# Inverse of the RWKV-7 chunk matrices: four block levels computed on the columns of the odd blocks only

## The chip, the cores and the metric

The kernel runs on one core of one Trainium2 chip. The metric is the device time of one execution in microseconds, as a median of several runs. The engines are called TensorE (PE), VectorE (DVE), ScalarE (ACT), GpSimd (POOL) and SyncE (SP, which only issues loads here).

## What is computed

The reference is a two-layer decoder trunk on 256 tokens of width 2048. Each layer has three head groups side by side (a gated linear recurrence, latent attention, RWKV-7 time mixing), an output projection and a SwiGLU feed-forward part. The part that matters here is the RWKV-7 state update, 8 heads of 64:

```python
def step(state, inp):
    r_t, w_t, k_t, v_t, kk_t, a_t = inp
    sa = jnp.einsum('bhvk,bhk->bhv', state, -kk_t)
    state = (state * w_t[:, :, None, :]
             + sa[..., :, None] * (kk_t * a_t)[..., None, :]
             + v_t[..., :, None] * k_t[..., None, :])
    return state, jnp.einsum('bhvk,bhk->bhv', state, r_t)
```

The kernel does it in 4 chunks of 64 tokens. Within a chunk the dependence of sa on earlier sa of the chunk is a unit lower triangular 64x64 matrix for each head, and it needs that matrix's inverse: 8 heads by 4 chunks, 32 inverses a layer.

## The kernel before

Two heads share the 128 partitions (rows 0 to 63 and 64 to 127), so a tile of 128 x 16 x 64 holds all 32 matrices; h8 is a half of it, 8 matrices wide. The inverse is built by doubling blocks. `inv` holds the inverse of the diagonal blocks of size m, `inv_t` its transpose. For m = 2, 4, 8, 16, 32 (RW_LEVELS, levels 0 to 4) and for each half:

1. GpSimd (L435) masks `mab` to the blocks below the diagonal that join two neighbouring blocks of size m (odd block of rows, even block of columns) into `rw_level`. It begins when TensorE has finished level_g of the level before (rw_gt_mm).
2. TensorE, level_g(k), multiplies `rw_level` (stationary) with `inv_t` (moving) into bank 0 or 1. L1715 is the line of the helper `both_heads`, two products for each of 8 matrices. An f32 product is two instructions, so a level_g or level_x with both halves is 64 instructions. L1724 is the helper for the last level.
3. ScalarE, gt_out(k) at L680, copies the bank into `g_t`.
4. TensorE, level_x(k), multiplies `inv` (stationary) with `g_t` (moving) into bank 2 or 3.
5. VectorE, level(k), subtracts the bank from `inv_t` (L1280) and transposes the result in 64x64 blocks into `inv` (L1272).

The last level (m = 32) already works on its quarters only. Every operation is released by semaphores, and the order on each engine is written out by hand. All engines have attention work between the levels. On TensorE the order is level_g(0), k_turn(1) (L1640), level_x(0), attend(1), attend(2) (L1670 and L1676), level_g(1), attend(3), level_x(1), p_turn(0), p_turn(1) (L1688), level_g(2), level_x(2), p_turn(2), p_turn(3), mix(0) (L1696 and L1697), level_g(3), mix(1), product, level_x(3), product, level_g(4), and so on. On VectorE it is k_norm(1) (L1171 and L1173), a small product at L1301, score_max(0) (addition L1183 of PSUM scores and mask, maxima L1186, small products L1190), level(0), score_max(1), probs(0) (reciprocal L1198, products L1202), score_max(2), probs(1), score_max(3), level(1), probs(2), probs(3), level(2), and so on. A score addition L1183 needs the attend of its pair of heads; p_turn needs probs of its pair.

Of the kernel before, what the change touches and what calls it, by code (L numbers as in the profile page):

```python
# [32 lines left out]
ACT = mybir.ActivationFunctionType  # L33
# [8 lines left out]
CH = 512  # L42
# [11 lines left out]
RC = 64  # L54
# [31 lines left out]
RW_LEVELS = [2, 4, 8, 16, 32]  # L86
# [26 lines left out]
def build(nc, stream, x_in, positions, params, consts, lora, gains, rows, out):  # L113
    with ExitStack() as ctx:
# [3 lines left out]
        def sem(name):  # L118
            return ctx.enter_context(nc.semaphore(name))
# [30 lines left out]
        def at(off, *shape):  # L150
            n = int(np.prod(shape))
            assert off + n <= ARENA
            v = arena[:, off:off + n]
            if len(shape) == 2:
                return v.rearrange("p (a b) -> p a b", b=shape[1])
            if len(shape) == 3:
                return v.rearrange("p (a b c) -> p a b c", b=shape[1], c=shape[2])
            return v
# [65 lines left out]
        rw_level = gain[:, 1024:2048].rearrange("p (n i) -> p n i", i=RC)  # L224
# [3 lines left out]
        g_t = at(RING_END + 9856, JC, RC)  # L228
        inv = at(RING_END + 10880, JC, RC)
        inv_t = at(RING_END + 11904, JC, RC)  # L230
# [10 lines left out]
        y_out = at(RING_END + 10880, 4, SEQ)  # L241
        UP_BANK = [4, 6, 4, 4, 6, 6, 4, 6]
        EVEN, ODD = slice(0, 64), slice(64, 128)

        UPPER = [slice(0, 32), slice(64, 96)]
        LOWER = [slice(32, 64), slice(96, 128)]

        psum = ctx.enter_context(nc.psum_tensor("psum", [P, 8, CH], F32))

        def bank(b, n=1):  # L250
            return psum[:, b:b + n, :].rearrange("p a b -> p (a b)")
# [36 lines left out]
        def S(name):  # L288
            if name not in names:
                names[name] = sem(name)  # L290
            return names[name]
# [151 lines left out]
        def _(act):  # L443
# [60 lines left out]
            for l in range(DEPTH):  # L504
# [164 lines left out]
                def gt_out(k):  # L669
                    last = k == len(RW_LEVELS) - 1  # L670
                    for hf in range(2):
                        h8 = slice(8 * hf, 8 * hf + 8)
                        act.wait_ge(S("rw_gt_mm"), 10 * l + 2 * k + hf + 1)
                        if last:
                            g3 = bank(hf).rearrange("p (n t) -> p n t", n=8)
                            nc.scalar.activation(g_t[UPPER[0], h8, 32:64], g3[UPPER[0], :, 32:64], ACT.Copy)
                            nc.scalar.activation(g_t[UPPER[1], h8, 32:64], g3[UPPER[1], :, 32:64], ACT.Copy).then_inc(
                                S("rw_gt_ready"), 1)
                        else:
                            nc.scalar.activation(g_t[:, h8, :].rearrange("p a b -> p (a b)"), bank(hf),  # L680
                                                 ACT.Copy).then_inc(S("rw_gt_ready"), 1)

                up_out(0)
                scaled(4, 12, 2, 0)
# [57 lines left out]
                nc.scalar.activation(rkT, bank(4)[:, 0:SEQ], ACT.Copy).then_inc(S("mla_rT_ready"), 1)  # L742
                stacked(1, b_st, 0)
                gt_out(0)
                k_out(1)
                softmax(0)
                softmax(1)
                gt_out(1)
                softmax(2)
                softmax(3)  # L750
                probs_out(0)
                probs_out(1)
                gt_out(2)
                probs_out(2)
                probs_out(3)
# [83 lines left out]
        def _(dve):  # L839
# [9 lines left out]
            def u(ins):  # L849

                steps[0] += 1
                ins.then_inc(chain, 1)

            def settle():

                dve.wait_ge(chain, steps[0])

            def vs(ins, name, value):

                ins.then_inc(S(name), 1)  # L860
                dve.wait_ge(S(name), value)

            tt, ts, stt = nc.vector.tensor_tensor, nc.vector.tensor_scalar, nc.vector.scalar_tensor_tensor
            red, rec, cp = nc.vector.tensor_reduce, nc.vector.reciprocal, nc.vector.tensor_copy
            ADD, SUB, MUL, MAX = ALU.add, ALU.subtract, ALU.mult, ALU.max
# [93 lines left out]
            for l in range(DEPTH):  # L959
# [73 lines left out]
                flat = "p h t -> p (h t)"  # L1033
# [236 lines left out]
                def turn_blocks(dst, src):  # L1270

                    return nc.vector.transpose(dst.rearrange("p n t -> p (n t)"), src.rearrange("p n t -> p (n t)"))  # L1272

                def level(k):
                    last = k == len(RW_LEVELS) - 1
                    for hf in range(2):
                        h8 = slice(8 * hf, 8 * hf + 8)
                        dve.wait_ge(S("rw_dinv_mm"), 10 * l + 2 * k + hf + 1)
                        if not last:
                            vs(tt(inv_t[:, h8, :], inv_t[:, h8, :], bank(2 + hf).rearrange("p (n t) -> p n t", n=8), SUB),  # L1280
                               "rw_xt", 12 * l + 2 * k + hf + 3)
                            vs(turn_blocks(inv[:, h8, :], inv_t[:, h8, :]), "rw_x", 10 * l + 2 * k + hf + 3)
                        else:
                            d3 = bank(2 + hf).rearrange("p (n t) -> p n t", n=8)
                            for up in UPPER:
                                z = inv_t[up, h8, 32:64]
                                u(tt(z, z, d3[up, :, 32:64], SUB))
                            settle()
                            dve.sem_inc(S("rw_xt"), 1)
# [11 lines left out]
                v(tt(md[:, :, 0:3], hd[:, :, 0:3], hd[:, :, 1:4], MUL))  # L1301
                score_max(0)
                level(0)
                score_max(1)
                probs(0)
                score_max(2)
                probs(1)
                score_max(3)
                level(1)
                probs(2)  # L1310
                probs(3)
                level(2)
                mix_lo(0)
                mix_lo(1)
# [125 lines left out]
        def _(pe):  # L1440
# [50 lines left out]
            for l in range(DEPTH):  # L1491
# [218 lines left out]
                def both_heads(b0, ns, left, right, w):  # L1710

                    last = None
                    for m, n in enumerate(ns):
                        for hp in (EVEN, ODD):
                            last = mm(bank(b0, 2)[hp, m * w:(m + 1) * w], left(hp, n), right(hp, n),  # L1715
                                      start=True, stop=True)
                    return last

                def quarters(b0, ns, left, right):

                    last = None
                    for m, n in enumerate(ns):
                        for h in range(2):
                            last = mm(bank(b0)[UPPER[h], m * RC + 32:(m + 1) * RC], left(h, n), right(h, n),  # L1724
                                      start=True, stop=True)
                    return last
# [5 lines left out]
                def tile_of(z):  # L1732
                    return lambda hp, n: z[hp, n, :]

                def unit_of(hp, n):
                    return idst[hp, :]

# [6 lines left out]
                def level_g(k):  # L1744
                    last = k == len(RW_LEVELS) - 1
                    pe.wait_ge(S("rw_level_ready"), 5 * l + k + 1)
                    for hf in range(2):
                        ns = range(8 * hf, 8 * hf + 8)
                        pe.wait_ge(S("rw_xt"), 12 * l + 2 * k + hf + 1)
                        if last:  # L1750
                            quarters(hf, ns, lambda h, n: rw_level[LOWER[h], n, 0:32],
                                     lambda h, n: inv_t[LOWER[h], n, 32:64]).then_inc(S("rw_gt_mm"), 1)
                        else:
                            both_heads(hf, ns, tile_of(rw_level), tile_of(inv_t), RC).then_inc(S("rw_gt_mm"), 1)

                def level_x(k):
                    last = k == len(RW_LEVELS) - 1
                    for hf in range(2):
                        ns = range(8 * hf, 8 * hf + 8)
                        pe.wait_ge(S("rw_gt_ready"), 10 * l + 2 * k + hf + 1)  # L1760
                        pe.wait_ge(S("rw_x"), 10 * l + 2 * k + hf + 1)
                        if not last:
                            both_heads(2 + hf, ns, tile_of(inv), tile_of(g_t), RC).then_inc(S("rw_dinv_mm"), 1)
                        else:
                            quarters(2 + hf, ns, lambda h, n: inv[UPPER[h], n, 0:32],
                                     lambda h, n: g_t[UPPER[h], n, 32:64]).then_inc(S("rw_dinv_mm"), 1)
# [12 lines left out]
                for t in range(TT):  # L1779
                    for j in range(4):  # L1780
                        n = 4 * t + j
# [135 lines left out]
                for n, (c, j) in enumerate(WO_ORDER):  # L1917
# [10 lines left out]
                    if n == 1:  # L1928
# [5 lines left out]
                        for m in range(JC):  # L1934
                            i, k = m % 4, m // 4
# [148 lines left out]
```

## Time and profile before

| | us |
|---|---|
| median of 3 runs | 2366.62 (2366.38 to 2368.61) |
| profiled execution | 2367.02 |
| its span | 2365.2 |
| TensorE busy | 2326.6 (98%) |
| VectorE busy | 1341.4 (57%) |
| ScalarE busy | 1082.8 (46%) |
| GpSimd busy | 64.3 (3%) |

The span is the time from the first to the last instruction. Busy is the time in which an engine has at least one instruction in work. The chain of waits goes back from the last instruction to whatever released it, so an operation on it is one whose length counts. TensorE holds 94% of that chain and VectorE 5%. The clock granted to TensorE is full in all 40 slices, and TensorE is busy for nine tenths or more in nearly all of them. The inverses lie between 299 and 347 us in layer 0 and between 1472 and 1521 us in layer 1.

### The profile page before, as it was taken

To read this page: it belongs to the slowest core of one execution; us is meant where nothing else is said; L and a number is where in the kernel's file an instruction comes from. 1 tells how busy PE (TensorE), PEld (TensorE's weight loads), DVE (VectorE), ACT (ScalarE), POOL (GpSimd) and SP (SyncE) were. 2 spreads that over 40 slices of the span, in tenths; PEclk is the share of its full clock that TensorE was granted. 3 is DMA by queue.
4 is the path that set the end of the run, shared out by engine and by line. 5 is a ranking of instruction groups with operands and counts; after the bars stand their busy time and mean duration, and the time that the engine had idled before them with its cause. 6 is when DMAs were issued, how large, how long until landed. Compare 5 with 4: busy or idle time off the path is not lost.

```text
span 2365.2 us, 34149 instructions
## 1 busy us (share of the span) xinstructions
PE 2326.6 (98%) x13908; PEld 1929.4 (82%) x13908; DVE 1341.4 (57%) x1369; ACT 1082.8 (46%) x1287; POOL 64.3 (3%) x67
## 2 busy tenths in 40 slices
PE   7999989999999999999999999999999999999999
PEld 6888678888888888888888886888888888888887
DVE  5696576644555444445556857675454554454454
ACT  5554654444443344444445546444444433444433
POOL 1000110000000000000000002100000000000000
PEclk9999999999999999999999999999999999999999
DMA  8453304655555555555454533055555555555553
GB/s 314 165 183 119 132 3 178 205 203 189 184 194 187 191 194 194 193 180 195 179 194 151 193 113 106 21 182 191 185 189 195 181 192 196 196 187 187 194 185 136
DMA packets 60179, 411.27 MB, mean 174 GB/s; under 512 B 6688, under 2 KB 6720, under 8 KB 13472
## 3 DMA queue, kind: packets, MB, share of 16 engines
q1 hardware_dynamic: 58624, 401.63, 47.2%
q0 software_dynamic: 1440, 7.97, 1.0%
q8 instruction: 88, 1.44, 0.2%
q14 instruction: 27, 0.22, 0.0%
HBM read 407.48 MB, written 2.10 MB: 173 GB/s over the span
## 4 chain that ended last, share of the span: by engine, by line
PE 94%; DVE 5%; issue 1%; ACT 0%; DMA 0%; DVEq 0%; POOL 0%; ACTq 0%; POOLq 0%
PE psum L1459 28%; PE psum L1461 28%; PE psum L1460 28%; PE psum L1620 2%; PE psum L1868 1%; PE psum L1715 1%; PE psum L1955 1%; PE psum L1470 1%; PE psum L1521 1%; DVE arena L1202 1%; DMA gain<-gains_dram 0%; DVE arena L1272 0%; DVE small L1186 0%; DVE arena L1183 0%; PE psum L1696 0%
## 5 line engine op out<-in xcount | busy, mean ns | idle before, releaser
L870 DVE TENSOR_TENSOR w_lo<-raw,w_hi 128x1024 fp32r<-128x1024 f32 (+2 forms) x752 | 901.6, 1205 | 841.6 <-ACT w_hi L453 834.7
L453 ACT ACTIVATE w_hi<-raw 128x1024 fp32r<-128x1024 f32 (+2 forms) x752 | 782.0, 1044 | 1099.2 <-PE psum L1461 1086.7
L1459 PE MATMUL psum<-w_hi,hT_hi 128*128 128x512 f32 (+2 forms) x2128 | 821.8, 386 | 3.8 <-DVE w_lo L870 2.5
L1461 PE MATMUL psum<-w_hi,hT_lo 128*128 128x512 f32 (+2 forms) x2128 | 816.6, 384 | 0.0
L1460 PE MATMUL psum<-w_lo,hT_hi 128*128 128x512 f32 (+2 forms) x2128 | 816.4, 384 | 0.0
L1459 PEld LDWEIGHTS psum<-w_hi,hT_hi 128*128 128x128 f32 x2128 | 399.8, 188 | 82.6 <-issue 2.5
L1461 PEld LDWEIGHTS psum<-w_hi,hT_lo 128*128 128x128 f32 x2128 | 399.8, 188 | 78.2
L1460 PEld LDWEIGHTS psum<-w_lo,hT_hi 128*128 128x128 f32 x2128 | 400.0, 188 | 76.5
L1459 PE MATMUL psum<-w_hi,act_hi 128*128 128x512 f32 x880 | 343.6, 390 | 0.0
L1461 PE MATMUL psum<-w_hi,act_lo 128*128 128x512 f32 x880 | 342.5, 389 | 0.0
L1460 PE MATMUL psum<-w_lo,act_hi 128*128 128x512 f32 x880 | 342.4, 389 | 0.0
L1461 PEld LDWEIGHTS psum<-w_hi,act_lo 128*128 128x128 f32 x880 | 165.2, 188 | 34.2
L1459 PEld LDWEIGHTS psum<-w_hi,act_hi 128*128 128x128 f32 x880 | 165.3, 188 | 34.0
L1460 PEld LDWEIGHTS psum<-w_lo,act_hi 128*128 128x128 f32 x880 | 165.3, 188 | 33.8
L1620 PE MATMUL psum<-raw,arena 128*128 128x384 f32 (+1 forms) x192 | 71.8, 525 | 2.0 <-ACT arena L634 1.3
L1620 PEld LDWEIGHTS psum<-raw,arena 128*128 128x128 f32 x192 | 35.4, 190 | 31.0 <-issue 13.7
L1393 DVE TENSOR_TENSOR act_lo<-psum,act_hi 128x1024 f32 (+1 forms) x22 | 26.9, 1225 | 37.8 <-ACT act_hi L820 37.8
L914 DVE TENSOR_TENSOR x<-x,psum 128x1024 f32<-128x1024 f32 x24 | 29.2, 1215 | 13.4 <-PE psum L1461 13.4
L1715 PE MATMUL psum<-arena 64*64 64x64 f32 x1024 | 32.4, 219 | 1.5 <-ACT arena L680 1.5
L1715 PEld LDWEIGHTS psum<-arena 64*64 64x64 f32 x1024 | 30.8, 135 | 3.4 <-ACT arena L680 1.8
L820 ACT ACTIVATE act_hi<-psum 128x1024 f32 (+1 forms) x22 | 22.6, 1028 | 20.8 <-PE psum L1955 20.8
L401 POOL TENSOR_TENSOR gain<-arena,row 128x128 f32<-128x128 f32 x2 | 0.9, 461 | 1034.2 <-PE psum L1604 1034.2
(312 smaller groups left out, 1213.0 us busy)
## 6 DMA issues: line engine op xcount, KB each, us to landing
raw<-stream_dram SPq DMA_DIRECT2D x360, 1024.0 KB, 4.8
raw<-stream_dram SPq DMA_DIRECT2D x16, 512.0 KB, 3.5
raw<-stream_dram SPq DMA_DIRECT2D x8, 768.0 KB, 4.5
raw<-stream_dram SPq DMA_DIRECT2D x8, 640.0 KB, 3.8
gain<-gains_dram POOLq DMA_DIRECT2D x3, 1024.0 KB, 6.9
x<-x_in_dram SPq DMA_DIRECT2D x4, 512.0 KB, 8.8
out_dram<-x SPq DMA_DIRECT2D x4, 512.0 KB, 5.5
lor<-lora_dram POOLq DMA_DIRECT2D x2, 832.0 KB, 12.0
```

The source lines that it names most:

```text
L453: nc.scalar.activation(w_hi[:, q % HALF_RING, 0:2 * w], raw[:, j % 4, hf * 2 * w:(hf + 1) * 2 * w], ACT.Copy).then_inc(hi_done, 1)
L870: tt(w_lo[:, q % HALF_RING, 0:2 * w], raw[:, j % 4, hf * 2 * w:(hf + 1) * 2 * w], w_hi[:, q % HALF_RING, 0:2 * w].bitcast(F32), SUB).then_ ...
L914: vs(tt(xs, xs, psum[:, b0:b0 + 2, :], ADD), "x_added", n_added)
L1202: u(tt(z, z, along(small[:, 64 + off + 2 * p:66 + off + 2 * p], n), MUL))
L1393: tt(act_lo[:, k, :], bank(4, 2).rearrange("p (k t) -> p k t", k=4), act_hi[:, k, :].bitcast(F32), SUB).then_inc(S("act_lo_ready"), 1)
L1459: mm(o, a_hi, w_hi[:, r, cols], start=(k == 0), stop=False)
L1460: mm(o, a_hi, w_lo[:, r, cols], start=False, stop=False)
L1461: last = mm(o, a_lo, w_hi[:, r, cols], start=False, stop=(k == n_k - 1))
L1470: last = tr(bank(x_turn_bank(n, c), 2)[:, k * SEQ + t * P:k * SEQ + (t + 1) * P], xg_tile(n, c)[:, t, k * P:(k + 1) * P], ident)
L1521: last = mm(bank(b0)[half, n * RC:(n + 1) * RC], left[:, h, tok], right[:, h, tok], start=True, stop=True)
L1620: last = mm(psum[:, UP_BANK[c] + t, 0:w], src[:, k, t * P:(t + 1) * P], raw[:, c % 4, k * w:(k + 1) * w], start=(k == 0), stop=(k == nk - 1))
L1715: last = mm(bank(b0, 2)[hp, m * w:(m + 1) * w], left(hp, n), right(hp, n), start=True, stop=True)
```

## The change

For a block of size m the level's correction is zero in the columns of even blocks. The change takes out these columns in levels 0 to 3. `odd_blocks` is a view of the odd blocks' columns (runs of m elements, each m elements apart), `level_bank` the first 256 columns of a bank, cut in runs of m. level_g and level_x have 32 moving columns for each matrix where they had 64, and write 32 columns each, packed into the first half of the bank. The eviction copies 256 columns of the bank into the odd blocks of `g_t`; the subtraction reads 256 columns of the bank and reads and writes the odd blocks of `inv_t`. The even blocks of `g_t` are neither written nor read. Numbers of instructions, semaphores, waits and the order on every engine stay as they were. The masks of GpSimd, the stationary operands and the transposes are the same, and level 4 is not touched.

```diff
+        def odd_blocks(z, k):
+            m = RW_LEVELS[k]
+            flat = z.rearrange("p n t -> p (n t)") if len(z.shape) == 3 else z
+            return flat.rearrange("p (b two m) -> p b two m", two=2, m=m)[:, :, 1, :]
+
+        def level_bank(b, k):
+            return psum[:, b, 0:CH // 2].rearrange("p (b m) -> p b m", m=RW_LEVELS[k])
...
-                            nc.scalar.activation(g_t[:, h8, :].rearrange("p a b -> p (a b)"), bank(hf),
-                                                 ACT.Copy).then_inc(S("rw_gt_ready"), 1)
+                            nc.scalar.activation(odd_blocks(g_t[:, h8, :], k), level_bank(hf, k), ACT.Copy).then_inc(
+                                S("rw_gt_ready"), 1)
...
-                            vs(tt(inv_t[:, h8, :], inv_t[:, h8, :], bank(2 + hf).rearrange("p (n t) -> p n t", n=8), SUB),
-                               "rw_xt", 12 * l + 2 * k + hf + 3)
+                            z = odd_blocks(inv_t[:, h8, :], k)
+                            vs(tt(z, z, level_bank(2 + hf, k), SUB), "rw_xt", 12 * l + 2 * k + hf + 3)
...
+                def odd_of(z, k):
+                    return lambda hp, n: odd_blocks(z[hp, n, :], k)
...
-                            both_heads(hf, ns, tile_of(rw_level), tile_of(inv_t), RC).then_inc(S("rw_gt_mm"), 1)
+                            both_heads(hf, ns, tile_of(rw_level), odd_of(inv_t, k), RC // 2).then_inc(S("rw_gt_mm"), 1)
...
-                            both_heads(2 + hf, ns, tile_of(inv), tile_of(g_t), RC).then_inc(S("rw_dinv_mm"), 1)
+                            both_heads(2 + hf, ns, tile_of(inv), odd_of(g_t, k), RC // 2).then_inc(S("rw_dinv_mm"), 1)
```

## Rows read from the trace of the kernel before

**Rows 1.** Busy time by stretch: length, PE, PEld, DVE, ACT, POOL, clock, DMA.
```profile
240.00:363.70 123.70, 114.00 (x1895) 89.72 (x1893) 83.61 (x118) 67.78 (x126) 23.12 (x11) 1.00 0.18 65
```
**Rows 2.** Chain that ended last, 290 to 376 us: start, length, what.
```profile
321.80 3.20 DVE arena L1202 x2
...
326.53 0.88 PE psum L1688 x6
...
334.86 5.75 PE psum L1715 x192
340.60 1.13 PE psum L1724 x64
```
**Rows 3.** Groups by form, VectorE, 299 to 350 us: busy, mean ns, idle before.
```profile
L1280 DVE TENSOR_TENSOR arena<-arena,psum 128x512 f32<-128x512 f32 x8 | 5.5, 687 | 0.6
...
L1202 DVE TENSOR_TENSOR arena<-arena,small 128x256 f32<-128x256 f32 x4 | 1.7, 425 | 0.1
...
L1287 DVE TENSOR_TENSOR arena<-arena,psum 32x256 f32<-32x256 f32 x4 | 1.7, 414 | 1.5 <-PE psum L1724 1.3
```
**Rows 4.** Instructions of line 1007: minimum, median, maximum ns; first and last start.
```profile
L1007 DVE TENSOR_TENSOR arena<-arena x8: 684/692/696, 131.3 to 1340.0; 128x512 f32<-128x512 f32 x8
```
**Rows 5.** Groups by form, ScalarE, 299 to 350 us.
```profile
L680 ACT ACTIVATE arena<-psum 128x512 f32<-128x512 f32 x8 | 4.5, 589 | 4.0 <-PE psum L1715 4.0
...
L676 ACT ACTIVATE arena<-psum 32x256 f32<-32x256 f32 x2 | 0.7, 372 | 3.4 <-PE psum L1724 3.4
```
**Rows 6.** TensorE: instructions of lines 1715 and 1724; then pieces of the chain.
```profile
L1715 PEld LDWEIGHTS psum<-arena x1024: 129/135/135, 290.8 to 1517.1; 64*64 64x64 f32 x171
L1715 PE MATMUL psum<-arena x1024: 218/218/267, 290.8 to 1517.1; 64*64 64x64 f32 x171
...
L1724 PEld LDWEIGHTS psum<-arena x128: 101/108/108, 345.5 to 1520.5; 32*32 32x32 f32 x128
L1724 PE MATMUL psum<-arena x128: 191/191/212, 345.5 to 1520.5; 32*32 32x32 f32 x128
...
259.76 1.68 PE psum L1782 x16
...
290.01 0.87 PE psum L1640 x8
...
330.03 2.01 PE psum L1715 x64
```
**Rows 7.** Timeline of layer 0: start, length, engine, line; in brackets the idle time before.
```profile
302.00 0.17 DVE L1301 TENSOR_TENSOR srw<-srw 128x12 f32<-128x12 f32 x1
...
302.38 2.37 POOL L435 TENSOR_TENSOR gain<-arena,con 128x1024 f32<-128x1024 f32 x1 [4.67 <-PE psum L1715]
...
306.77 0.93 PE L1676 MATMUL psum<-arena 64*128 64x128 f32 x8
...
307.92 0.96 DVE L1183 TENSOR_TENSOR arena<-psum,con 128x768 f32<-128x768 f32 x1
...
309.96 0.23 DVE L1190 SCALAR_TENSOR_TENSOR small<-small 128x2 f32<-128x2 f32 x2
...
312.16 2.36 POOL L435 TENSOR_TENSOR gain<-arena,con 128x1024 f32<-128x1024 f32 x1 [7.41 <-PE psum L1715]
...
313.81 0.80 DVE L1190 SCALAR_TENSOR_TENSOR small<-small 128x2 f32<-128x2 f32 x2
...
322.06 2.38 POOL L435 TENSOR_TENSOR gain<-arena,con 128x1024 f32<-128x1024 f32 x1 [7.54 <-PE psum L1715]
...
322.70 2.08 PE L1715 MATMUL psum<-arena 64*64 64x64 f32 x64 [0.74 <-ACT arena L680]
```
**Rows 8.** Timeline of layer 1, the same columns.
```profile
1475.85 0.17 DVE L1301 TENSOR_TENSOR srw<-srw 128x12 f32<-128x12 f32 x1
1475.87 2.38 POOL L435 TENSOR_TENSOR gain<-arena,con 128x1024 f32<-128x1024 f32 x1 [4.67 <-PE psum L1715]
...
1481.43 0.96 DVE L1183 TENSOR_TENSOR arena<-psum,con 128x768 f32<-128x768 f32 x1
```

## Prediction

> **What bounds the kernel now.** I read the stretch table first, then the chain of waits inside one RWKV stretch, then the timeline of its engines, and last the durations by form.
>
> The stretch from 240.0 to 363.7 us is the only one of its layer in which TensorE has holes, with the clock at full speed throughout [rows 1]. In the streamed products before and behind it TensorE has work all the time, and an edit inside the inverse cannot reach them. So the question is what the chain does between 300 and 363 us. The chain lies on VectorE from 301 to 326.5 us: softmax work and the inverse's updates in one queue, one after the other, the long L1202 at 321.80 among them. From 326.53 us it lies on TensorE without a hole up to 345.6 us (attention products, three 64-instruction blocks in one piece of 192, the 32x32 blocks) [rows 2]. An operation of the inverse counts only if it is on the engine that leads at that moment. TensorE is close behind VectorE in the first part: its last attend(1) products begin at 306.77 us and end at 307.70, and the score addition that needs them starts at 307.92 [rows 7].
>
> **VectorE updates.** Four levels, two halves, two layers: 16 subtractions at L1280 of 128x512 at 0.686 us [rows 3]. They become 128x256. Two rows price that: L1287 is the same subtraction with 256 elements, at 0.414, and L1202 with 256 columns takes 0.425 [rows 3]. I take 0.42, so 0.27 less each, 0.54 a level, 1.07 for each layer's two levels on VectorE's part of the chain (levels 0 and 1) and nothing for levels 2 and 3, unless they are on the path. L1287 has runs of 32 elements, the new one runs of 2, 4, 8 and 16. L1007 settles whether short runs cost VectorE: it multiplies every other block of 32 down to 1 element in three operands, and all of its instructions lie at 684 to 696 ns [rows 4], the time of the contiguous L1280. The transposes at L1272 stay as they are.
>
> **ScalarE evictions.** 16 at L680, 0.589 us for 512 columns; with 256 columns in runs of 32 the row is 0.372 [rows 5], so 0.22 less each. Bounds: 0.37 if short runs are free, 0.6 if they cost double. Only in level 2 is TensorE seen waiting for one: its block at 322.70 stood 0.74 us idle for L680 [rows 7]. A gain there lets level_x(2) end about 0.25 earlier, near 324.5 us, and p_turn(2) behind it waits for VectorE at 325.0 anyway. So the eviction by itself is worth nothing, but it is what lets TensorE follow when VectorE arrives earlier.
>
> **TensorE products.** 1024 instructions (two passes of 32 products for each of 8 blocks, two layers) go from 64 moving columns to 32. A block of 64 takes 2.01 us, 31.4 ns each [rows 6]. The upper bound of the gain is the 32x32 block, 1.13 us for 64, 17.7 ns each [rows 2]: 0.9 us a block. But there the weights are half as wide too. The weight loads last 135 and 108 ns for 64 and 32 weight columns [rows 6], so about 0.83 ns a column. A full-width product with 2 moving columns comes every 105 ns and one with 128 every 109 [rows 6]: with weights that wide the load sets the pace and moving columns are free. For 64 weight columns a load streams 53 ns; two heads in different halves of the array alternate, so no product can come faster than every 27 ns, and 1.72 us for a block is the floor. Since 64 moving columns stream for the same 53 ns, loads and products are balanced today, and halving one leaves the other. I take no change of pace, between 0 and 0.3 us a block, nearest to the 105-against-109 rows; only the drain of a block's last product gets shorter, by 27 ns (218 to 191) [rows 6].
>
> The Trainium skill, TensorEngine Tiling (Array Packing), "Instruction Overhead", speaks against this part of the change: a product has some 60 cycles of overhead, so one with a single column is as slow as one with 60, and nothing is won from a dimension that is already small. By that rule the pace would stay near today's, and the sum below would be the same. The 17.7 ns of the 32x32 rows show that small products can run faster than 60 cycles at 2.4 GHz (25 ns), so here it is the load, not that floor, on which I rest.
>
> **What of it reaches the end.** Layer 0, level 0: VectorE would be 0.57 us earlier at the score addition of 307.92 (0.54, and a little drain), but attend(1) ends at 307.70 and its release takes 0.09, so it starts at 307.79: 0.13 is left. Even that is then lost. GpSimd's mask of the next level runs 312.16 to 314.52, gated by TensorE's level_g(1), and the small L1190 at 313.81 takes 0.80 instead of the 0.23 at 309.96, ending at 314.61, just behind it [rows 7]. Whatever VectorE gains ahead only lengthens that wait. Level 0 is worth 0.03, the drain. Layer 1 shows the same picture, with the addition at 1481.43 [rows 8] 0.15 us behind the end of attend(1).
>
> Level 1 is behind that wait and in front of the next: its 0.54 and 0.03 of the drain move everything up. The long L1202 at 321.80 (3.19 us for one of 256 and one of 512 columns, where 256 take 0.425 [rows 3]) is another wait for GpSimd, whose mask runs 322.06 to 324.44. That mask starts when level_g(2) ends, and this follows VectorE's own L1280, so both move together and the collision stays as it is, 0.57 earlier. TensorE takes over at 326.53 minus 0.57, and from there its work is the same.
>
> Levels 2 and 3 run beside TensorE's unbroken 326.5 to 345.6 us: they are worth nothing. That cover is 1.07 us if it were gone.
>
> Sum: 0.03 + 0.57 = 0.6 us a layer, 1.2 in two. The profiled execution has a span of 2365.2 in 2367.02 us; it becomes 2365.8, and as the median lies 0.40 under it, 2366.62 becomes 2365.4.
>
> **Rivals.**
> A. The products do get faster, at the 27 ns floor: 0.3 us a block. Then level_g(3) and level_x(3), which are on TensorE's part, give 0.6, and attend(1) and the mask of 312.16 come 0.6 to 0.9 earlier, so that level 0's 0.57 is freed too: 1.75 a layer, 3.5 in all, 2363.1. For it: the measured 31 ns are above 27. Against: full-width weight loads show no faster pace with 2 columns than 105.
>
> B. GpSimd gets between. In layer 1 VectorE's L1301 starts at 1475.85 and GpSimd's mask at 1475.87 [rows 8]; the mask starts behind level_g(0), so a slightly shorter block puts it first. L1202 and L1190, products of SBUF operands, stood until the mask beside them was done [rows 2, 7], so L1301, of the same kind, would. The mask seems to block only some 0.15 us after its start (the first L1202 was not held), so the block must shrink by about 0.15; in layer 0, with starts of 302.00 and 302.38 [rows 7], by 0.5. Price: L1301 waits 2.1 us, of which level 0's 0.54 and the vanished wait of L1190, 0.8 in layer 1, pay back 1.35: 0.8 us more than the forecast, 2366.2. The Trainium skill, SBUF — State Buffer, "SBUF: two separate sides", states this lock: whichever of the two starts first holds the shared port pair for its whole instruction, and the other fully blocks. By that rule the collision would go to the first starter.
>
> C. Slower: TensorE reads its moving operand in runs of two words (level 0), and may take longer over them. No row of before has such a read. The load covers up to 53 ns a product, so 32 columns may cost twice their 0.83 ns for nothing; from there it costs. At four times, 107 ns a product and 54 an instruction, level 0's two blocks grow by 1.4 us each, 2.9 a layer on TensorE, which then leads: +2.3 after the 0.57, 2371.3 in all; if all four levels suffered, about 10 us a layer, 2386.
>
> D. VectorE or ScalarE pay double for short runs: the change does nothing, 2366.6.
>
> **Chances.** Forecast 0.62, A 0.14, B 0.10, D 0.08, C 0.06. The range holds the forecast, A, B and D with half a microsecond at A's end and, at the other, the 2 us by which one of three runs of before lay above the others: 2362.6 to 2368.5. A measurement of this kernel tells some 0.2% (4.7 us) from no change. Faster by that needs the 17.7 ns pace without any collision: 0.02. Slower needs C: 0.05. Within: 0.93.
>
> **What would show it.** L1280 at 0.42 and L680 at 0.37 us; a 64-instruction block at L1715 still near 2.0 us; L1190 of the third score pair waiting longer than 0.80; the long L1202 still about 3.2 and some 0.6 earlier; TensorE's unbroken part unchanged in length. A block under 1.8 us is rival A, one over 2.1 rival C, a 2 us L1301 in layer 1 rival B. The argument fails if the gain of level 0 survives to 318 us, or if TensorE shows new holes behind 326 us.

## The result and the profile after

The changed kernel takes 2375.24 us in the median (2372.55 to 2378.56) where before took 2366.62 (2366.38 to 2368.61 in the first runs). The ratio is 1.0034, with a 95% interval of 1.0024 to 1.0045. Forecast were 2365.4 us and a range of 2362.6 to 2368.5. So the change makes the kernel slower, by about 8 us, and the measured time lies outside the range. The profiled execution of after took 2373.01 us with a span of 2371.2, 6.0 over the span of before.

The groups by form of the changed kernel, 299 to 350 us (busy, mean ns, idle before), show that the subtraction and the eviction did what they should. The lines that answer to [rows 3, 5] are L1292 and L691 now:

```profile
L1292 DVE TENSOR_TENSOR arena<-arena,psum 128x256 f32<-128x256 f32 x8 | 3.4, 421 | 0.6
...
L691 ACT ACTIVATE arena<-psum 128x256 f32<-128x256 f32 x8 | 2.9, 383 | 4.4 <-PE psum L1726 4.4
```

The timeline of layer 0 (start, length, engine, line; idle time before in brackets) answers to [rows 7]. `both_heads` is L1726, the masks are L446, the score addition L1194, the small products L1201, the long products L1213:

```profile
300.10 2.05 PE L1726 MATMUL psum<-arena,gain 64*64 64x32 f32 x64 [0.59 <-DVEq L1307]
...
307.65 0.96 DVE L1194 TENSOR_TENSOR arena<-psum,con 128x768 f32<-128x768 f32 x1 [0.43 <-PE psum L1687]
...
311.96 2.37 POOL L446 TENSOR_TENSOR gain<-arena,con 128x1024 f32<-128x1024 f32 x1 [7.36 <-PE psum L1726]
...
313.54 0.88 DVE L1201 SCALAR_TENSOR_TENSOR small<-small 128x2 f32<-128x2 f32 x2
...
318.98 2.23 PE L1726 MATMUL psum<-arena,gain 64*64 64x32 f32 x64 [1.03 <-DVE arena L1292]
...
321.08 3.18 DVE L1213 TENSOR_TENSOR arena<-arena,small 128x256 f32<-128x256 f32 x2
...
321.30 2.40 POOL L446 TENSOR_TENSOR gain<-arena,con 128x1024 f32<-128x1024 f32 x1 [6.97 <-PE psum L1726]
...
322.30 3.30 PE L1726 MATMUL psum<-arena 64*64 64x32 f32 x64 [1.09 <-ACT arena L691]
...
325.54 2.82 PE L1699 MATMUL psum<-con,arena 128*128 128x128 f32 x12
```

Up to 322.3 us this is the forecast, line by line. A block of halved products (64 instructions) keeps its 2.05 us. The score addition now waits 0.43 us for attend(1), the small products wait longer for the mask (0.88 where it was 0.80), and the long L1213 starts 0.72 earlier with its collision intact (0.11 of that lies ahead of the inverse, which starts at 300.10 instead of 300.21). But the next block, level_x(2), takes 3.30 us where the same instructions took 2.06 eight microseconds before, and the transposes behind it (L1699, 12 in 2.82 us) start every 0.21 us where before they started every 0.11. The stretch table says why (columns as in [rows 1]: length, PE, PEld, DVE, ACT, POOL, granted clock, DMA share, GB/s):

```profile
300.00:318.00 18.00, 17.77 (x324) 14.88 (x324) 15.94 (x33) 10.45 (x30) 4.74 (x2) 1.00 0.01 3
318.00:322.30 4.30, 2.23 (x64) 2.05 (x65) 3.95 (x11) 3.94 (x12) 1.00 (x1) 1.00 0.00 0
322.30:329.30 7.00, 7.00 (x80) 6.74 (x81) 5.48 (x9) 1.84 (x3) 1.41 (x1) 0.53 0.01 2
329.30:349.00 19.70, 19.61 (x558) 18.61 (x557) 9.30 (x12) 7.21 (x11) 2.36 (x1) 0.99 0.01 3
349.00:354.00 5.00, 4.02 (x85) 4.05 (x87) 2.74 (x5) 1.33 (x2) 0.00 (x0) 0.66 0.02 3
...
1495.00:1508.00 13.00, 12.01 (x153) 11.31 (x154) 8.54 (x16) 5.57 (x14) 2.50 (x1) 0.61 0.00 1
...
1526.00:1532.00 6.00, 4.93 (x116) 4.89 (x114) 2.90 (x5) 1.33 (x2) 0.00 (x0) 0.72 0.01 3
```

TensorE's granted clock falls from 1.00 to 0.50, from its level of 2.4 GHz to that of 1.2, four times in the two layers: from 322.7 to 329.6 and from 350.0 to 353.4 us, and in layer 1 from 1496.9 to 1507.2 and from 1527.6 to 1531.0. The first of each pair lies at level 2, the second in the state loop behind the inverse. In the profile of before it stays at 1.00 from the first inverse to 2364 us. (In the last two microseconds of the span it falls in every profile here, before's included.) A row of 40 slices is too coarse to see this: a slice is 59 us long, a digit 9 stands for 0.90 or more, the two falls of layer 0 leave it at 9, and those of layer 1 make it an 8. Here is the same table of the kernel before:

```profile
318.00:322.30 4.30, 2.44 (x66) 2.05 (x64) 3.95 (x11) 3.75 (x11) 0.24 (x1) 1.00 0.00 0
322.30:329.30 7.00, 5.72 (x89) 5.19 (x90) 6.57 (x9) 2.45 (x4) 2.14 (x1) 1.00 0.01 2
...
349.00:354.00 5.00, 4.98 (x170) 4.85 (x168) 3.19 (x4) 1.72 (x4) 0.00 (x0) 1.00 0.03 8
```

The whole difference of the spans lies in these stretches. From the start of level_g(0) to that of the piece of three blocks it is 34.58 us in before (300.21 to 334.79) and 36.25 in after, 1.67 more; from there to the first streamed product 28.89 and 29.96, 1.07 more. In layer 1 the two parts cost 2.44 and 0.84 more. Together that is 6.02, against 6.0 us between the spans. The falls at level 2 cost 4.11 of it, with the gain of VectorE already taken off, and the parts with the late falls 1.91.

### The profile page after: what moved, and what is told of

Read it like the earlier page. It is cut to its first block, busy times and chain, and to the rows that moved or that the text cites. A ratio compares the mean times of both kernels' runs of the same rounds, so it can differ in the third digit from the quotient of the medians.

```text
span 2371.2 us, 34149 instructions
## 1 busy us (share of the span) xinstructions
PE 2335.5 (98%) x13908; PEld 1938.7 (82%) x13908; DVE 1336.4 (56%) x1369; ACT 1079.5 (46%) x1287; POOL 64.4 (3%) x67
## 4 chain that ended last, share of the span: by engine, by line
PE 95%; DVE 3%; ACT 1%; issue 0%; DMA 0%; DVEq 0%; POOL 0%; ACTq 0%; POOLq 0%
PE psum L1470 28%; PE psum L1472 28%; PE psum L1471 28%; PE psum L1631 2%; PE psum L1726 2%; PE psum L1882 1%; PE psum L1969 1%; PE psum L1481 1%; PE psum L1532 1%; PE psum L1707 0%; DMA gain<-gains_dram 0%; DVE arena L1304 0%; DVE small L1197 0%; DVE arena L1194 0%; PE psum L1699 0%
## 5 line engine op out<-in xcount | busy, mean ns | idle before, releaser
L1726 PE MATMUL psum<-arena 64*64 64x32 f32 (+1 forms) x1024 | 35.1, 227 | 1.7 <-ACT arena L691 1.7
L1726 PEld LDWEIGHTS psum<-arena 64*64 64x64 f32 x1024 | 33.6, 145 | 3.6 <-ACT arena L691 1.9
```

## Theory and experiments

**Theory.** The products kept their pace, but each has half the moving columns, and so, it is argued, keeps the array at work for half the time; the profile has no measure of that work. Around level 2, where TensorE also stands idle twice for about 1 us, what is left does not keep the full clock. **Rivals.** The clock falls because VectorE and ScalarE are done earlier and TensorE's idle times move; or the strided read of the moving operand is at fault (the prediction's C); or only the number of halved products counts, wherever they stand.

In the diffs below HALF_LEVELS names the levels whose products have 32 moving columns. In the others they have 64 and fill the bank, and ScalarE and VectorE take the odd blocks out of the full bank. The mean clock is that over the span, with the runs' range: one fall of 3.4 us takes 0.0007 off it, one of 6.8 us 0.0014, so that 1.000 means that no such fall came.

**1. Everything but TensorE's part.**

```diff
+HALF_LEVELS = ()
 def level_bank(b, k):
+    if k not in HALF_LEVELS:
+        return odd_blocks(psum[:, b, :], k)
...
-both_heads(hf, ns, tile_of(rw_level), odd_of(inv_t, k), RC // 2)
+both_heads(hf, ns, tile_of(rw_level), odd_of(inv_t, k), width(k))   # 64 outside HALF_LEVELS
```

> All of the change for ScalarE and VectorE, none for TensorE: the products keep 64 moving columns and fill the whole bank, the eviction and the subtraction take only the odd blocks' columns, now in runs of m out of PSUM. Theory 1 (the halved moving columns lower TensorE's activity, and its granted clock falls): no stretch between 300 and 365 us below clock 1.00, L1292 at 0.42 us, the block of level_x(2) back at 2.08 us, median some 1 us under before, near 2365.5 us. Rival (the earlier VectorE and ScalarE work moves TensorE's idle times, and that makes the clock fall): the clock falls at 322 us as in the changed kernel, 2372 us or more. Second rival (two-word runs are slow for the engines): L1292 above 0.6 us.

Measured: 2366.95 us, before beside it 2367.91; ratio 0.9998 (0.9989 to 1.0007), mean clock 0.998 to 1.000. The subtraction takes 0.422 us, now out of runs of two words in PSUM. The stretch of the table, and the block that had gone slow:

```profile
322.30:329.30 7.00, 6.44 (x94) 5.75 (x96) 5.45 (x9) 1.81 (x3) 1.38 (x1) 1.00 0.01 2
...
322.27 2.08 PE L1729 MATMUL psum<-arena 64*64 64x64 f32 x64 [1.06 <-ACT arena L694]
```

Up to level 2 of layer 0, TensorE's instructions start within 0.1 us of those of after, with the same idle times in front of the two blocks of level 2 (1.04 and 1.06 here, 1.03 and 1.09 there), and the clock stays at 1.00 in both inverses. The timing of VectorE and ScalarE is not the cause of the falls at level 2. From level_g(0) to the piece of three blocks it is 34.04 us, 0.54 less than before, and in layer 1 34.12 against 34.66, again 0.54 less. That is the gain that the forecast put at 0.6 a layer, and the median is too coarse to show its sum.

One fall is left in this profile, of 3.4 us (1520.7 to 1524.1), in layer 1's state loop, where after has its last one. The row is one microsecond of it:

```profile
1522.00:1523.00 1.00, 1.00 (x24) 1.00 (x23) 0.34 (x1) 0.37 (x2) 0.00 (x0) 0.50 0.06 16
```

From the piece of three blocks to the first streamed product layer 1 takes 30.29 us here, 0.87 more than before's 29.42, and that is more than the 0.54 won ahead. No product is halved in this kernel. So the late fall of layer 1 is not shown to come from the halved columns; the profiles of the kernels with levels 0 and 1, 3, or 0, 1 and 3 halved (below) have it too, at 1521 to 1526 us.

**2. TensorE's part with the old timing of the others.** Small copies stand in front of each eviction and subtraction.

```diff
+nc.scalar.activation(pad[:, n0:n0 + 8], bank(hf)[:, 0:8], ACT.Copy)
 nc.scalar.activation(odd_blocks(g_t[:, h8, :], k), level_bank(hf, k), ACT.Copy)
...
+v(cp(pad[:, 128:128 + 96], bank(2 + hf)[:, 0:96]))
 z = odd_blocks(inv_t[:, h8, :], k)
```

> The changed kernel with small extra copies out of PSUM in front of each subtraction (96 columns, VectorE) and each eviction (8 columns, ScalarE), so that VectorE and ScalarE take about the time of before for a level while the products stay halved. Theory 1 (activity of TensorE): clock at 0.5 behind level_g(2) near 322 us and again near 350 us, 2371 to 2378 us. Rival (timing of VectorE and ScalarE): clock stays at 1.00 and the time is near 2366.6 us.

Measured: 2375.4 us (2374.54 to 2377.44), ratio 1.0033 (1.002 to 1.0046), mean clock 0.993 to 0.995. The added copy takes 0.257 us, so that the two halves of a level start 1.49 us apart on VectorE where before they started 1.46 apart, and TensorE's idle times at level 2 in layer 0 are near the old ones (1.32, 0.28 and 0.56 us; before 1.30, 0.23 and 0.74). The loss is all there without the gain in time. The falls of its profile are not quite those of after: 323.6 to 330.4 us, none near 350, then 1477.3 to 1487.5 (around levels 0 and 1 of layer 1), 1501.2 to 1511.4 and 1531.9 to 1535.3; the expected fall near 350 did not come. Together with experiment 1: at level 2 the halved columns bring the clock down, at either timing of the other engines.

**3. Which levels.** Only HALF_LEVELS changes.

> Halved moving columns in levels 0 and 1 only; levels 2 and 3 with 64 columns as before; VectorE and ScalarE as in the change. Theory 1, if what counts is the sparse stretch around level 2 (TensorE idle some 2 us between 318 and 324 us): no fall of the clock, near 2365.5 us. If the halved blocks of levels 0 and 1 alone are enough, the clock falls near 320 us or earlier and the time is 2370 us or more.

> Halved moving columns in level 2 only (four half blocks of 16 products a layer, 319 to 324 us), the rest with 64. Theory 1, place matters: the clock falls at 322 us as in the changed kernel and the time is 2369 us or more. If the number of halved blocks matters instead, one level in four is not enough: clock 1.00, near 2365.5 us.

> Halved moving columns in level 3 only, where TensorE has work without a hole (326 to 346 us); 64 columns in levels 0 to 2; VectorE and ScalarE as in the change. If the clock falls only where halved products meet TensorE's idle times around level 2, it stays at 1.00 up to 346 us and the median is near 2366 to 2367 us, as with full columns. If any halved level is enough, 2370 us or more.

> Halved moving columns in levels 0, 1 and 3, 64 in level 2. If the clock falls only where halved products stand between TensorE's idle times, at level 2, the clock stays at 1.00 up to 346 us, mean clock 0.999 to 1.000, near 2366.5 us, although three quarters of the halving are in. If the sum of the halving counts, 2370 us or more.

> Halved in levels 2 and 3. If the rest of the loss (8 us in the full change, 4 with level 2 alone) comes from level 3, whose halved products then follow a fall of the clock and keep it down or bring the late one, 2374 us or more; if not, 2371 us as with level 2 alone.

> Halved in levels 0, 1 and 2. If the rest of the loss comes from levels 0 and 1, by an earlier or a more frequent fall in front of level 2, 2374 us or more, with a mean clock of 0.995 or less; if not, 2371 us and 0.997.

| halved levels | median us | ratio to before (95%) | mean clock |
|---|---|---|---|
| none | 2366.95 | 0.9998 (0.9989 to 1.0007) | 0.998 to 1.000 |
| 0, 1 | 2367.06 | 1.0000 (0.9991 to 1.0009) | 0.997 to 1.000 |
| 3 | 2366.78 | 0.9999 (0.9990 to 1.0009) | 0.999 to 1.000 |
| 0, 1, 3 | 2366.49 | 0.9994 (0.9985 to 1.0003) | 0.999 to 1.000 |
| 2 | 2371.44 | 1.0016 (1.0006 to 1.0025) | 0.995 to 0.997 |
| 2, 3 | 2370.47 | 1.0008 (0.9999 to 1.0018) | 0.996 to 0.997 |
| 0, 1, 2 | 2374.9 | 1.0031 (1.0022 to 1.0041) | 0.993 to 0.996 |
| 0, 1, 2, 3 (the change) | 2375.24 | 1.0034 (1.0024 to 1.0045) | 0.993 to 0.996 |

Place decides, not number. Three levels of four cost nothing when level 2 is left alone; level 2 alone loses half; levels 0 and 1 add the other half, but only with level 2; level 3 adds nothing anywhere. (The row of levels 2 and 3 has an interval that just takes in no change; its mean clock, 0.996 to 0.997 in all ten executions, is near that of level 2 alone.) Levels 0 and 1 lie just in front of level 2 (300 to 318 us); level 3 lies behind the fall, in work without a hole. Rows of the stretch table, for levels 0, 1 and 3 halved, then for 0, 1 and 2:

```profile
322.30:329.30 7.00, 6.44 (x94) 5.75 (x96) 5.49 (x9) 1.84 (x3) 1.42 (x1) 1.00 0.01 2
```

```profile
322.30:329.30 7.00, 6.98 (x80) 6.71 (x81) 5.50 (x9) 1.86 (x3) 1.43 (x1) 0.54 0.01 2
349.00:354.00 5.00, 3.97 (x83) 4.00 (x85) 2.75 (x5) 1.33 (x2) 0.00 (x0) 0.66 0.01 3
1496.00:1508.00 12.00, 11.40 (x140) 10.65 (x137) 7.62 (x15) 4.61 (x11) 2.53 (x1) 0.57 0.00 1
```

The second kernel has the falls of the full change, one for one. With level 2 alone, or 2 and 3, the profiles have a fall of 6.8 us at level 2 in each layer, and neither a late one in either layer nor the 3.4 us by which the one in layer 1 is longer. So in the profiles levels 0 and 1 add to the loss by making that fall longer and by late falls. How they do it stays open, the more so as a late fall in layer 1 comes with no level halved as well.

**4. Strided reads.** Only level 2 is halved, and its products read 32 columns in one run.

```diff
 def odd_of(z, k):
-    return lambda hp, n: odd_blocks(z[hp, n, :], k)
+    if k not in HALF_LEVELS:
+        return tile_of(z)
+    return lambda hp, n: z[hp, n, 0:RC // 2]
```

> Like the run with only level 2 halved, but the products of level 2 read the first 32 columns of each matrix in one run instead of the odd block of 8 columns in four; the inverse of level 2 is then wrong. Theory (fewer moving columns are what counts, however they are read): the clock falls at 322 to 325 us as there, 2370 to 2373 us. Rival (the strided read of the moving operand is what costs): clock 1.00, near 2366.5 us.

Measured: 2371.47 us, ratio 1.0017 (1.0007 to 1.0026), against 1.0016 with the strided read. The clock falls in the same place:

```profile
318.00:322.00 4.00, 2.29 (x65) 2.05 (x64) 3.65 (x11) 3.52 (x11) 0.58 (x1) 1.00 0.00 0
322.00:330.00 8.00, 7.58 (x82) 7.33 (x83) 5.90 (x9) 2.25 (x5) 1.82 (x1) 0.57 0.01 2
```

At level 2 the number of moving columns is what counts, not how they are read. Rival C has fallen as a mechanism: its two-word reads at level 0 cost no pace either (2.05 us a block in after). Which of level 2's two steps, level_g or level_x, is needed for the fall was not tried.

**5. What sets the pace of the products.** Sixteen moving columns in levels 0 and 1.

```diff
+def width(k):
+    return RC // 4 if k < 2 else RC // 2
...
+    return lambda hp, n: odd_blocks(z[hp, n, :], k)[:, 0:width(k) // RW_LEVELS[k], :]
```

> The changed kernel with 16 moving columns in place of 32 in levels 0 and 1: half of the odd blocks is left out, the eviction and the subtraction read the same quarter of a bank twice, and the inverse is not computed. If the weight loads set the pace, the blocks of levels 0 and 1 stay at 2.0 us for 64 instructions although the columns are a quarter of before. If the moving columns still counted, about 1.6 us or less. The clock: at 0.5 behind 322 us as in the changed kernel, and possibly already between 300 and 318 us, if a still smaller activity is enough to lose it there.

Measured: one time of 2376.65 us, mean clock 0.994. The first two blocks of the inverse:

```profile
301.29 2.04 PE L1732 MATMUL psum<-arena,gain 64*64 64x16 f32 x64 [0.59 <-DVE arena L1289]
...
304.29 2.04 PE L1732 MATMUL psum<-arena 64*64 64x16 f32 x64
```

With 64, 32 and 16 columns a block takes 2.08, 2.06 and 2.04 us: the columns are free. That the weight loads set the pace in their place can be read from the starts of single instructions. The instructions of the two heads start in pairs, 7 ns apart, and a pair comes every 58 ns with 64 weight columns (59 with 64 moving columns, 58 with 32 and 16). In the 32x32 block of before (L1724) a pair comes every 32 ns, and the full-width L1782, with only 2 moving columns, every 112 ns. So 128, 64 and 32 weight columns give 112, 58 and 32 ns, the last two with 32 moving columns each. These rows differ in their partitions, too; no run was made that varied the weights alone.

In layer 0 the clock stayed full up to 323 us even so; in layer 1 it was at 0.50 from 1477.0 to 1490.7 us, around levels 0 and 1. The smaller width is not shown to be the reason, since experiment 2, with 32 columns, has a fall from 1477.3 us as well.

**6. Work in the idle times.** The changed kernel, and products of the identity with itself where TensorE waits.

```diff
+def fill(b, n):
+    for i in range(n):
+        mm(bank(b)[:, 0:P], ident, ident, start=True, stop=True)
 def level_g(k):
+    if k == 2:
+        fill(0, 4)
...
 def level_x(k):
+    if k == 2:
+        fill(2, 4)
...
 if c == 0:
+    fill(1, 4)
```

The last two lines, behind the first products of the state loop, are only in the kernels that are filled there, and of those the ones filled "in the state loop" have only them.

> The changed kernel, all four levels halved, with four products of the identity with itself (128x128, about 0.87 us) in front of level_g(2) and four in front of level_x(2), where TensorE waits 1.03 and 1.09 us; their result is overwritten. Theory (activity of TensorE over the stretch decides): the clock stays at 1.00 around 322 us and the time comes back to some 2366 us, up to 2369 us where the later fall at 350 us remains. Rival (something in the halved products themselves, such as their strided reads or short outputs, brings the clock down): the clock falls at 322 us all the same, 2372 us or more.

> The changed kernel with filling products at all three places. Theory (the falls of the clock are all of what the change loses): clock 0.999 to 1.000 in the mean, some 2 us less than with the filling in level 2 alone, 2367 to 2369 us. If a loss remains with the clock at 1.000, something else is lost, too.

> Full moving columns in all levels, VectorE and ScalarE on the odd blocks, and the same filling products at three places: both of level 2 and, four of them, in the hole of 1.07 us behind the first products of the state loop (347 to 348.4 us). Theory: the occasional fall of the clock near 350 and 1520 us, which the runs with full columns show too, goes away; every run lies near 2365.5 us with a spread below 1.5 us, 0.1% under before. Rival: the filling delays real work, 2367 us or more.

> Full moving columns, VectorE and ScalarE on the odd blocks, and the four filling products only in the hole behind the first products of the state loop. Theory: layer 0 from level_g(0) to the first streamed product takes 62.7 us as in the run with full columns (63.5 before) and layer 1 the same, since the late fall of the clock does not come; the median is 1.5 to 2.5 us under that of before. Rival: the filled kernel with full columns was slower for a reason other than the clock, and this one is too, 2367 us or more.

> The kernel before with the four filling products in the hole behind the first products of the state loop alone. Theory: its slower runs (2368 to 2371 us) are those in which the clock falls there; with the filling all lie within 1.5 us, and the median is under before's by up to 1 us. Rival: the spread has another cause and stays.

| kernel | median us (range) | ratio to before (95%) | mean clock |
|---|---|---|---|
| change, filled at level 2 | 2371.32 (2369.03 to 2373.29) | 1.0018 (1.0009 to 1.0027) | 0.997 to 1.000 |
| change, filled at all three places | 2371.11 (2365.56 to 2373.87) | 1.0014 (1.0005 to 1.0023) | 0.997 to 1.000 |
| full columns, filled at all three | 2368.69 (2365.97 to 2372.86) | 1.001 (1.0 to 1.0019) | 0.999 to 1.000 |
| full columns, filled in the state loop | 2367.63 (2365.88 to 2369.55) | 0.9999 (0.999 to 1.0008) | 0.998 to 1.000 |
| before, filled in the state loop | 2368.89 (2366.67 to 2370.87) | 1.0006 (0.9997 to 1.0015) | 0.998 to 1.000 |

With level 2 alone filled, the clock of the profiled execution is full in both inverses, with all four levels halved. It has two falls of 3.4 us elsewhere: one at 17.6 us, long before the first inverse, and one at 1522.9, in layer 1's state loop:

```profile
318.00:324.00 6.00, 5.80 (x98) 5.10 (x96) 5.61 (x13) 4.39 (x14) 1.16 (x1) 1.00 0.01 3
324.00:331.00 7.00, 6.42 (x100) 5.75 (x98) 5.33 (x9) 1.74 (x4) 1.26 (x1) 1.00 0.00 0
1519.00:1529.00 10.00, 8.89 (x265) 8.56 (x263) 5.00 (x10) 2.35 (x3) 0.00 (x0) 0.83 0.01 3
```

In the profiled execution of the second kernel, filled at all three places, the clock is full up to 2364 us and the span is 2364.5 us, 0.7 under that of before:

```profile
318.00:322.30 4.30, 4.16 (x82) 3.67 (x80) 3.98 (x10) 3.98 (x12) 1.04 (x1) 1.00 0.01 4
322.30:329.30 7.00, 6.41 (x96) 5.74 (x96) 5.45 (x9) 1.80 (x3) 1.38 (x1) 1.00 0.00 0
349.00:354.00 5.00, 4.98 (x170) 4.85 (x168) 2.41 (x4) 2.10 (x4) 0.00 (x0) 1.00 0.03 8
```

So the same halved products run at full clock where other work stands between them. But of the eleven executions of this kernel only two were at a mean clock of 1.000 (2365.56 and 2366.28 us); nine were at 0.997 or 0.998 and at 2370.07 to 2373.87. The filling takes back half of the loss, and it does not do so reliably. Against the unfilled change the mean clock rose from 0.993 to 0.996 to 0.997 and above. Both expectations on the time, up to 2369 and 2367 to 2369 us, were missed. Where the clock fell in the nine executions isn't known, since the one that was profiled is one of the two at 1.000. Part of what is left may be the filling itself: with full columns and the same three places filled the median is 2368.69, 2.08 us over before's beside it, at a mean clock of 0.999 to 1.000.

The three kernels with full columns or of before do not gain from filling, and their expectations of 2365.5 us, of 1.5 to 2.5 us under before and of a spread below 1.5 us were all missed. Those with it spread as much as those without, also among executions with a mean clock of 1.000 (2365.97 to 2372.8 us with all three places filled). So a fall of the clock does not make all of the spread. It goes with the slow end of it: before was run 114 times beside the other kernels, and all eleven of its executions above 2369.1 us (up to 2371.73) have a mean clock of 0.998 or 0.999, while of the other 103 only three are under 1.000. The filling in the state loop did not take such executions away: its four slowest of eleven (2370.38 us and up) are at 0.998 or 0.999 too. Where in them the clock falls no profile shows. What makes the rest of the spread stays open. One part can be read in the profiles: the first products of the gated recurrence come at 102.97 us in before and at 104.54 in before with filling, long before either inverse, and many of before's executions lie near 2366.2 or near 2368.1 us, all with the full clock.

No version was measurably faster than before. The fastest median beside its before was that with levels 0, 1 and 3 halved, 2366.49 against 2367.89 us, with an interval (0.9985 to 1.0003) that takes in no change.

## Why the prediction was wrong

**The view that failed** was the first one. "With the clock at full speed throughout [rows 1]" was read as a property of the stretch; it was a result of the work in it. No rival asked whether the change could take it away, though it halves what TensorE's array does in 512 instructions a layer. The part "What bounds the kernel now" treated TensorE as busy or waiting, and the change hardly alters that: the busy time of TensorE from 318.0 to 322.3 us is 2.44 us before and 2.23 after.

**The step that failed** is the last of "What of it reaches the end": "TensorE takes over at 326.53 minus 0.57, and from there its work is the same". It has the same instructions, but at half the clock from 322.7 to 329.6 us. The sum put the way from level_g(0) to the piece of three blocks at 0.6 us less a layer. It is 1.67 us more in layer 0 and 2.44 in layer 1, and behind it, where the sum had nothing, another 1.07 and 0.84. With all products at 64 columns it is 0.54 less, as forecast.

**What held.**
- The subtraction: 0.42 forecast, 0.421 measured. The eviction: 0.37 and 0.383. L1007's rows were good evidence for short runs, and D has fallen.
- The pace of the products: no change forecast, 2.08 to 2.06 us measured, and 2.04 with a quarter of the columns. The reading of the 105-against-109 rows (L1782 with 2 moving columns, L1640 with 128) was right as to the columns, and A has fallen.
- The rule of the Trainium skill in that part (TensorEngine Tiling (Array Packing), "Instruction Overhead": 60 cycles of overhead for a small product) would have given the same pace. The trace agrees that columns below some 60 are free, down to 16, but the rule's 60 cycles (25 ns) are not the pace: each half of the array gets an instruction every 58 ns. The prediction's argument against the rule as a floor does not hold: 17.7 ns is the mean over two instructions that start 7 ns apart in two halves, and each half has one every 32 ns.
- The path: level 0's gain is lost against attend(1) and the mask; level 1's arrives; levels 2 and 3 are covered. With full columns a layer gained 0.54 up to the piece of three blocks, where 0.60 was forecast.
- B did not happen: in layer 0 the mask of level 1 starts at 302.24 us, 0.36 behind L1312's 301.88. In layer 1 it was as close as it can be: both start at 1478.55, and L1312 takes its 0.17 us all the same. B's 0.15 us does not come out of its row: the first L1202 started 0.25 us ahead of the mask, so it says nothing of a product that starts behind one. The rule of the Trainium skill on the shared port pair (SBUF — State Buffer, "SBUF: two separate sides": the first starter holds it for its whole instruction, the other waits) agrees with the forecast collisions on VectorE's side: the products that start beside a running mask, at 313.54 and behind the one of 321.08, end only after it. That the mask in its turn waits for a product begun before it doesn't show: the mask of 321.30 overlaps the first long product by 0.20 us and takes 2.40, against 2.37 elsewhere.

One detail was off without effect: level_x(2) was to be held by nothing but its eviction. The chain of the changed kernel does go there over ScalarE, but over its softmax work in front of the eviction (start, length, what):

```profile
318.36 2.23 ACT arena L658 x8
320.59 1.39 ACT arena L665 x2
321.98 0.28 ACT arena L691
322.26 0.04 issue
322.30 3.30 PE psum L1726 x64
```

With VectorE 0.5 us faster, ScalarE comes level with it. By this chain a further gain on VectorE in level 1 would have to pass ScalarE; no run tried it.

**Rival C** gave 2371.3 us, the right sign at a chance of 0.06, for a reason that the unchanged 2.05 us of a block and the contiguous read exclude. That it has the right sign is luck. The chance of slower, 0.05, was too low since it rested on that one mechanism.

The Trainium skill has a rule that the prediction did not weigh: TensorE: Matmul & The Clock Gate, "What's actually happening", says that a block of hardware watches how busy TensorE has been and sets its clock to one of two levels, and that the low one is what it gets without enough work. The trace agrees as to the levels: 1.00 and 0.50 and nothing between. Had a fall of 7 us in each layer been weighed, in which TensorE's work on the path takes twice its time, it would have been priced at 3.5 us a layer less the 0.6 won, some 2372 us. That is an estimate made afterwards, from the measured length of the fall; nothing in the rows of before gives the length or the place.

## What to carry to other kernels

An edit that takes moving columns out of TensorE's instructions without making them faster wins nothing there, and may cost the clock of what stands behind it. Before such an edit, look for the places where TensorE already has idle times of a microsecond, and leave the products there as they are; here the same edit in a dense stretch (level 3) was harmless. And a granted clock of 1.00 in the profile of before is a measurement of that kernel's work in that execution, not a constant to carry over: 14 of 114 executions of before itself are under 1.000.

## What the runs showed of the hardware

- The 128 instructions of level 2 in a layer, with 32 instead of 64 moving columns and idle times of 1.0 and 1.1 us in front of their two blocks, were enough to bring the granted clock from 1.00 to 0.50 for 6.8 us, in each layer of the profiled execution, and the mean clock to at most 0.997 in every one of ten executions. Idle time alone does not tell it: before has 1.30, 0.23 and 0.74 us of it in the same place at full clock.
- Once down at level 2, the clock of the changed kernel stayed at 0.50 for 6.8 us in layer 0, while TensorE was busy without a hole (7.00 of 7.00 us), and for 10.2 us in layer 1; the falls in the state loop lasted 3.4 us. The loss outlasts its cause: in layer 0 the clock falls 0.4 us after level_x(2) has begun, so the first block of level 2 ran at full clock, and the second, the transposes and the attention products behind it paid.
- What is lost depends on what went before: levels 0 and 1 halved are harmless alone and double the loss of level 2 (2371.44 to 2374.9 us).
- The clock can fall in the state loop with no product halved: 1520.7 to 1524.1 us in the profile of experiment 1, behind an idle time of 1.07 us. Before has that idle time too, and in its profile no fall.
- A product with 64 weight columns in two alternating halves of the array costs the same 32 ns an instruction with 64, 32 or 16 moving columns (blocks of 64 in 2.08, 2.06 and 2.04 us). The two halves take theirs 7 ns apart, and the next pair comes after 58 ns; with 32 weight columns after 32, and with 128, on the whole array, one comes after 112.
- VectorE reads runs of two words, eight bytes apart, out of PSUM at the pace of packed ones (0.420 to 0.423 us for 256 columns over all four levels, packed 0.421).
